# Modulation weights before rows in the first stage, and rows turned by products with diag(1/norm)

## The chip, the core and the metric

The kernel runs on one core of a Trainium2 chip. The time is device microseconds (us) of one execution, the median over the runs. The core has TensorE (PE, matrix products), VectorE (DVE), ScalarE (ACT), GpSimd (POOL), SyncE (SP, which here issues the loads) and DMA engines, all running on their own and tied by semaphores.

## The reference

One block of a hybrid network: four sequence mixers over 1,280 tokens (256 of context, 1,024 of the sequence; 1,024 channels), and then a mixture of experts. What matters here is how the mixers' input is made:

```python
def rms_norm(x, g):
    xf = x.astype(jnp.float32)
    y = xf * lax.rsqrt(jnp.mean(xf * xf, axis=-1, keepdims=True) + RMS_EPS)
    return (y * g.astype(jnp.float32)).astype(x.dtype)

def modulate(x, g, shift, scale):
    return rms_norm(x, g) * (1 + scale) + shift
...
        mod_x = jax.nn.silu(c) @ w_mod[i] + b_mod[i]
        mod_c = jax.nn.silu(c_ctx) @ w_mod[i] + b_mod[i]
        sa_x, ca_x, ga_x, sf_x, cf_x, gf_x = jnp.split(mod_x[:, None, :], 6, axis=-1)
        sa_c, ca_c, ga_c, sf_c, cf_c, gf_c = jnp.split(mod_c[None, None, :], 6, axis=-1)
        y_c, ctx_states = mixer_block(modulate(ctx, norm1_g[i], sa_c, ca_c), ctx_init, lp, 1, n_ctx)
        y_x, _ = mixer_block(modulate(x, norm1_g[i], sa_x, ca_x), ctx_states, lp, rows, GRID_W)
```

## The kernel before, in words

All data are float32. The kernel is a chain of stages, each a `Phase` that ends with a barrier of all engines. The first stage is `front`, the second `gla` (one of the mixers); seven more follow, in which the change alters nothing.

`front` makes `k.hT`, the modulated input with channels on the partitions: 8 chunks of 128 channels by 1,280 tokens. The tokens come as ten tiles `X[:, t]` of 128 rows by 1,024 channels, two of context and eight of the sequence. The order on each engine is the order in which the code is written.

- SP loads the two conditions `c` and `c_ctx`, the ten row tiles (512 KB each), the first two of the six sections of `w_mod` in eight loads of 1 MB (two loads, a piece of 2 MB, for each pair of the eight chunks of input channels), and the vectors `b_mod` and `norm1_g`.
- ACT takes the Silu of the conditions and then sums the squares of each row tile (line 248).
- DVE makes the reciprocal roots for five tiles at a time (`rsqrt`, twelve dependent small instructions after line 291 has formed the means) and scales the five tiles in place with them (line 294). This is done twice.
- PE multiplies the conditions with each weight piece as it lands (line 264, four output strips), turns the result into columns (line 270) after DVE has copied it out (line 297), and DVE forms the gain and shift columns (lines 303 to 309). Then PE turns the scaled rows by transposes (line 281), in three groups of two, four and four tiles, eight channel chunks each, chunk `c_` into bank `c_`. ACT evicts banks 0 to 3 (line 253) and DVE banks 4 to 7 (line 314), applying gain and shift. A bank is refilled when its last eviction is out.

In `gla`, SP loads the low-rank weights `WG`, four loads of the q/k weights `W[0]`, the gate weights, and the v/g weights `W[1]`. PE computes the low-rank products (line 473: 512, 512 and 256 tokens), which DVE evicts (line 665), and then the q/k products (line 516).

Of the kernel before, what the change touches and what calls it, by code (L numbers as in the profile page):

```python
# [70 lines left out]
class Chain:  # L71
# [123 lines left out]
def front(nc, k, ctx, cr, x, ctx_in, c, c_ctx, w_mod, b_mod, norm1_g):  # L195
# [9 lines left out]
        sem("mod_rows_done"), sem("mod_rows_out"), sem("mod_columns_turned"), sem("mod_columns_out"), sem("front_chain"))  # L205
    W = cr.take(2, KC, D)
    X = cr.take(NT, D)
    R = cr.take(512)
    sc = cr.take(KC, 32)
    cc = cr.take(2, KC)  # L210
    bcol, gcol, modc = cr.take(6, KC), cr.take(KC), cr.take(2, KC, 2)
    ss, rs, ri, rt = (cr.take(NT) for _ in range(4))
    junk = k.hT[:, 0, 0:D]
    ps = k.ps
    wv = w_mod[0].rearrange("(p c) (s n) -> s p c n", c=KC, s=6)
    tiles = [ctx_in[0, t * P:(t + 1) * P, :] for t in range(CT)] + [x[0, t * P:(t + 1) * P, :] for t in range(XT)]
    BATCH = NT // 2
    groups = [(1, 0, CT), (0, CT, CT + 4), (0, CT + 4, NT)]
    by_channel = lambda w, c_, h: w[:, c_, :].rearrange("p (q m) -> p m q", m=KC)[:, 4 * h:4 * h + 4, :]
    with nc.Block() as block:  # L220
# [17 lines left out]

        @block.scalar
        def _(act):  # L240
            act.wait_ge(c_in, 32)
            act.wait_ge(zeroed, 1)
            nc.scalar.activation(sc[:, :, 0:2].rearrange("p c j -> p j c"), cc, ACT.Silu).then_inc(act_in, 1)
            for t in range(NT):
                act.wait_ge(x_in[t], 16)
                if t >= 1:
                    act.wait_ge(sq, t)
                nc.scalar.activation(junk, X[:, t], ACT.Square, accum_out=ss[:, t:t + 1]).then_inc(sq, 1)
            act.wait_ge(cols_out, 4)
            for g, (j, a, b) in enumerate(groups):  # L250
# [33 lines left out]
        @block.vector  # L284
        def _(dve):
            chain = Chain(dve, vch)

            for n in range(2):
                b = slice(n * BATCH, (n + 1) * BATCH)
                dve.wait_ge(sq, (n + 1) * BATCH)  # L290
                chain(nc.vector.tensor_scalar(rs[:, b], ss[:, b], 1.0 / D, RMS_EPS, ALU.mult, ALU.add))
                rsqrt(nc, chain, rs[:, b], ri[:, b], rt[:, b])
                for t in range(n * BATCH, (n + 1) * BATCH):
                    nc.vector.tensor_scalar(X[:, t], X[:, t], ri[:, t:t + 1], None, ALU.mult).then_inc(xn_ready, 1)
# [16 lines left out]
            for g, (j, a, b) in enumerate(groups):  # L311
                for c_ in range(KC // 2, KC):
                    dve.wait_ge(turned, g * KC + c_ + 1)
                    nc.vector.tensor_scalar(k.hT[:, c_, a * P:b * P], ps[c_][:, 0:(b - a) * P],
                                            k.mul_col[0][j][:, c_:c_ + 1], k.add_col[0][j][:, c_:c_ + 1],
                                            ALU.mult, ALU.add).then_inc(out[1], 1)
# [57 lines left out]
def gla(nc, k, ctx, cr, w_in, gate_w2, gate_b, norm_g, ahead):  # L374
# [6 lines left out]
    W0 = cr.take(KC, 2 * GW)  # L381
# [8 lines left out]
    WG, low_end = cr.take(KC, 32), cr.at  # L390
# [8 lines left out]
    wg_in, qk_in, vg_in, w2_in = (sem("low_w_loaded"), [sem(f"qk_w_{c}_loaded") for c in range(KC // 2)],  # L399
                                  sem("vg_w_loaded"), sem("gate_w_loaded"))  # L400
# [33 lines left out]
    with nc.Block() as block:  # L434
        @block.sync
        def _(sp):
            sp.dma_start(WG, view[:, :, A_GL:A_GL + 32]).then_inc(wg_in, 16)
            for c in range(KC // 2):
                cs = slice(2 * c, 2 * c + 2)
                sp.dma_start(W[0][:, cs], view[:, cs, A_Q:A_Q + 2 * GW]).then_inc(qk_in[c], 16)  # L440
# [26 lines left out]
        def _(pe):  # L467
            pe.wait_ge(wg_in, 16)
# [38 lines left out]
            for p in range(NPROD):  # L507
# [5 lines left out]
                for c in range(KC):  # L513
                    if p == 0 and c % 2 == 0:
                        pe.wait_ge(qk_in[c // 2], 16)
                    last = nc.tensor.matmul(k.ps[p % 4][:, 0:width], k.hT[:, c, t * P:(t + 1) * P], W[g][:, c, ws],  # L516
                                            start=(c == 0), stop=(c == KC - 1))
# [2636 lines left out]
class Turn:  # L3154
# [556 lines left out]
def block_kernel(nc, io, out):  # L3711
    ctx = ExitStack()
    with ctx:
# [27 lines left out]
        with Phase(nc) as c:  # L3741
            left = gla(nc, k, c, at(free), io["w_in"], io["gla_gate_w2"], io["gla_gate_b"], io["gla_norm_g"], for_mamba)
# [58 lines left out]
```

## Time and profile before

| | us |
|---|---|
| Time, median of 3 runs | 2637.87 (2637.47 to 2639.95) |
| Profiled execution, its time | 2639.51 |
| Its span, first to last instruction | 2637.8 |
| Last square starts | 16.99 |
| Fourth burst of modulation products starts | 37.58 |
| Turning of rows starts, ends | 44.05, 53.25 |
| First product of `gla` starts | 58.93 |
| First q/k product starts | 67.87 |

Starts are counted from the span's start. "PE idle" in a row is the time before the instruction in which the engine had nothing to do, with the instruction or transfer that ended it. A float32 product is listed as two MATMUL records, a transpose as one. Over the whole span the mean granted clock of TensorE is 0.968 of full speed.

### The profile page before, as it was taken

How to read it: one execution, taken by the hardware profiler on the slowest of the kernel's cores; microseconds unless marked ns; L12 is line 12 of the kernel's file. 1: busy time of each engine (PE TensorE's matmuls, PEld its weight loads, DVE VectorE, ACT ScalarE, POOL GpSimd, SP SyncE). 2: the span in 40 equal slices, each digit the busy share in tenths (PEclk: the TensorE clock that was granted, in tenths of full speed). 3: DMA queues.
4: the chain of work that ended last, by engine and by line, in shares of the span. 5: the costliest groups of instructions: out<-in, count | busy, mean ns of one | idle time of the engine just before them, and what ended most of it. 6: DMA issues, size and time to landing. Idle time of an engine off the chain costs nothing. (4 is left out here: it accounts for less than half of the span.)

```text
span 2637.8 us, 72412 instructions
## 1 busy us (share of the span) xinstructions
PE 2434.2 (92%) x27309; PEld 1316.8 (50%) x27310; DVE 1504.5 (57%) x2601; ACT 967.0 (37%) x1642; POOL 827.8 (31%) x655
## 2 busy tenths in 40 slices
PE   4998999999799898999697978999999999999977
PEld 2446458555799455999443443333333333333333
DVE  3106556754577424676434855666666666666538
ACT  3513116312222123333111134555555555555422
POOL 1000000000454001111000035566666666666564
PEclk9999999999999999999798989999999999999988
DMA  6001312130000200000322277899989898693177
GB/s 249 26 0 53 129 32 68 49 112 1 13 4 4 56 12 1 4 4 4 122 93 80 88 293 286 336 351 365 352 311 363 325 336 333 231 337 131 66 297 300
DMA packets 109435, 410.21 MB, mean 156 GB/s; under 512 B 20954, under 2 KB 37036, under 8 KB 84141
## 3 DMA queue, kind: packets, MB, share of 16 engines
q1 hardware_dynamic: 76972, 289.81, 30.1%
q0 software_dynamic: 20736, 75.51, 7.4%
q10 hardware_dynamic: 11520, 41.95, 4.1%
q8 instruction: 154, 2.52, 0.4%
q14 instruction: 53, 0.43, 0.1%
HBM read 347.45 MB, written 59.77 MB: 154 GB/s over the span
## 5 line engine op out<-in xcount | busy, mean ns | idle before, releaser
L3367 PE MATMUL bank<-arena 128*32 x1280 | 570.2, 599 | 11.9 <-SPq L68 8.0
L3369 PE MATMUL bank<-arena 128*32 128x512 f32 x3840 | 571.3, 599 | 0.0
L3328 POOL COPY arena<-arena 128x2048 f32 x240 | 448.8, 1903 | 335.9 <-PE bank L3401 314.6
L3367 PEld LDWEIGHTS bank<-arena 128*32 128x32 f32 x1280 | 135.1, 110 | 362.0 <-issue 353.1
L3398 PE MATMUL bank<-arena 128*32 x640 | 290.4, 597 | 5.5 <-POOL arena L3328 5.5
L3401 PE MATMUL bank<-arena 128*32 128x512 f32 x1920 | 291.4, 597 | 0.0
L3522 DVE COPY arena<-arena 128x2048 f32 x80 | 133.6, 1670 | 208.9 <-PE bank L3369 190.8
L3459 ACT COPY arena<-arena 128x2048 f32 x80 | 152.0, 1900 | 176.7 <-PE bank L3369 149.7
L3318 POOL DMA_INDIRECT arena<-normed_rows,arena x80 | 164.0, 2050 | 119.2 <-DVE arena L3506 107.4
L1313 PE MATMUL bank<-arena 64*64 64x64 f32 x4480 | 164.8, 219 | 12.5 <-DVE arena L1385 5.4
L3398 PEld LDWEIGHTS bank<-arena 128*32 128x32 f32 x640 | 70.6, 110 | 198.5 <-issue 197.5
L1313 PEld LDWEIGHTS bank<-arena 64*64 64x64 f32 x4480 | 150.3, 135 | 17.9 <-DVE arena L1385 6.5
L3465 ACT COPY arena<-arena 128x2048 f32 x80 | 151.9, 1898 | 0.0
L3369 PEld LDWEIGHTS bank<-arena 128*32 128x32 f32 x3840 | 151.1, 110 | 0.0
L3500 DVE TENSOR_SCALAR arena<-bank,arena 128x128 f32<-128x128 f32 x320 | 109.3, 404 | 40.7 <-PE bank L3352 40.7
L1554 PE MATMUL bank<-arena 128*128 128x512 f32 (+1 forms) x320 | 132.0, 569 | 0.0
L516 PE MATMUL bank<-arena 128*128 128x512 f32 (+1 forms) x320 | 127.3, 552 | 0.0
L3434 ACT ACTIVATE arena<-bank,arena 128x128 f32<-128x128 f32 x320 | 120.9, 465 | 3.5 <-PE bank L3352 3.5
L2552 POOL TENSOR_TENSOR arena<-arena 128x512 f32<-128x512 f32 x10 | 12.8, 1282 | 345.3 <-DVE arena L2618 231.6
L1432 DVE SCALAR_TENSOR_TENSOR arena<-arena 128x945 f32<-128x945 f32 (+2 forms) x96 | 113.8, 1220 | 1.7
L2837 PE MATMUL bank<-arena 128*128 128x512 f32 x256 | 112.0, 595 | 0.0
L1385 DVE TENSOR_TENSOR arena<-arena,bank 128x512 f32<-128x512 f32 x100 | 68.5, 685 | 68.3 <-PE bank L1313 67.7
(558 smaller groups left out, 4327.5 us busy)
## 6 DMA issues: line engine op xcount, KB each, us to landing
arena<-in_exp_w_gate_dram SPq DMA_DIRECT2D x64, 1024.0 KB, 6.2
arena<-in_exp_w_up_dram SPq DMA_DIRECT2D x64, 1024.0 KB, 8.7
arena<-in_exp_w_down_dram SPq DMA_DIRECT2D x64, 1024.0 KB, 9.7
expert_rows<-arena ACTq DMA_DIRECT2D x80, 512.0 KB, 8.6
arena<-in_w_mod_dram SPq DMA_DIRECT2D x32, 512.0 KB, 4.4
arena<-in_x_dram SPq DMA_DIRECT2D x16, 512.0 KB, 5.6
arena<-in_w_mod_dram SPq DMA_DIRECT2D x8, 1024.0 KB, 18.5
arena<-in_w_in_dram SPq DMA_DIRECT2D x4, 1536.0 KB, 10.2
```

The source lines that it names most:

```text
L516: last = nc.tensor.matmul(k.ps[p % 4][:, 0:width], k.hT[:, c, t * P:(t + 1) * P], W[g][:, c, ws], start=(c == 0), stop=(c == KC - 1))
L1313: last = self.nc.tensor.matmul(self.banks[bank][r, x * HD:(x + 1) * HD], lhsT[r, x], rhs[r, x], start=True, stop=True)
L1554: last = nc.tensor.matmul(k.ps[p % 4][:, 0:w], W[m // 3 % 2][:, c, (m % 3) * P:(m % 3 + 1) * P], k.hT[:, c, a:a + w], start=(c == 0), stop ...
L3318: nc.gpsimd.indirect_dma_start(out=G[:, b.q], out_offset=None, in_=xn_dram, in_offset=bass.IndirectOffsetOnAxis(ap=ID[:, b.q], axis=0)).th ...
L3328: last = nc.gpsimd.tensor_copy(down_copy(u), down_of(slots[u]))
L3367: nc.tensor.matmul(out(SUB - 1), XTT[:, b.q, c, rows(SUB - 1)], W[:, :, c], start=first, stop=end)
L3369: last = nc.tensor.matmul(out(u), XTT[:, b.q, c, rows(u)], WC[:, u, :, c], start=first, stop=end)
L3398: nc.tensor.matmul(ps[6 + half][rows(SUB - 1), :], HT[:, b.q, f, rows(SUB - 1)], W[:, f, c], start=(f == 0), stop=(f == 1))
L3401: last = nc.tensor.matmul(ps[6 + half][rows(u), :], HT[:, b.q, f, rows(u)], WDC[:, u, f, c], start=(f == 0), stop=(f == 1))
L3459: nc.scalar.copy(copy_of(2, LOW), part_of(slot, LOW)).then_inc(lo_a, 1)
L3465: nc.scalar.copy(copy_of(2, HIGH), part_of(slot, HIGH)).then_inc(hi_a, 1)
L3522: nc.vector.tensor_copy(copy_of(0, LOW), part_of(slots[0], LOW))
```

## The change

In `front`, SP now issues the modulation weights and the two vectors first, then the ten row tiles, and then weights for `gla`: the low-rank weights at once, and the four q/k loads when the modulation products are done. For this the buffers of rows and small tiles get other places in the arena, and `gla` gets its `WG` and `W0` from outside. The rows are no longer scaled. DVE instead makes for each tile a 128x128 diagonal `DG[:, t]` of reciprocal norms, and PE turns and scales a tile in one product of `X[:, t, c_::KC]` with it. The tiles are in four groups of 2, 3, 3 and 2 instead of three; ACT and DVE do the squares and reciprocals of group g+1 before they evict group g, and DVE forms no reciprocals before the modulation columns are out.

```diff
     W = cr.take(2, KC, D)
-    X = cr.take(NT, D)
-    R = cr.take(512)
...
-    junk = k.hT[:, 0, 0:D]
+    X = Carve(cr.arena, cr.at + 3 * D + 80).take(NT, D)
+    R, junk, DG = small.take(512), small.take(D), small.take(NT, P)
...
-    BATCH = NT // 2
-    groups = [(1, 0, CT), (0, CT, CT + 4), (0, CT + 4, NT)]
+    groups = [(1, 0, CT), (0, CT, CT + 3), (0, CT + 3, CT + 6), (0, CT + 6, NT)]
...
-            for t in range(NT):
-                sp.dma_start(X[:, t], tiles[t]).then_inc(x_in[t], 16)
             for c_ in range(KC // 2):
                 cs = slice(2 * c_, 2 * c_ + 2)
                 for s in range(2):
                     sp.dma_start(W[:, s, cs], wv[s][:, cs]).then_inc(first_in[c_], 16)
             sp.dma_start(bcol, b_mod.rearrange("a (s p c) -> p (a s) c", s=6, c=KC)).then_inc(vec_in, 16)
             sp.dma_start(gcol, norm1_g.rearrange("a (p c) -> p (a c)", c=KC)).then_inc(vec_in, 16)
+            for t in range(NT):
+                sp.dma_start(X[:, t], tiles[t]).then_inc(x_in[t], 16)
+            sp.dma_start(next_low, view[:, :, A_GL:A_GL + 32]).then_inc(next_in, 16)
+            sp.wait_ge(rows_done, 1)
+            for c_ in range(KC // 2):
+                cs = slice(2 * c_, 2 * c_ + 2)
+                sp.dma_start(next_w[:, cs], view[:, cs, A_Q:A_Q + 2 * GW]).then_inc(next_in, 16)
+            sp.wait_ge(next_in, 16 * (1 + KC // 2))
...
+            squares(*groups[0][1:])
+            act.wait_ge(cols_out, 4)
+            for g in range(len(groups)):
+                if g + 1 < len(groups):
+                    squares(*groups[g + 1][1:])
+                leave(g)
...
                     for t in range(a, b):
-                        last = nc.tensor.transpose(ps[c_][:, (t - a) * P:(t - a + 1) * P], X[:, t, c_::KC], k.ident)
+                        last = nc.tensor.matmul(ps[c_][:, (t - a) * P:(t - a + 1) * P], X[:, t, c_::KC], DG[:, t],
+                                                start=True, stop=True)
                     last.then_inc(turned, 1)
...
-            for n in range(2):
-                b = slice(n * BATCH, (n + 1) * BATCH)
-                dve.wait_ge(sq, (n + 1) * BATCH)
-                chain(nc.vector.tensor_scalar(rs[:, b], ss[:, b], 1.0 / D, RMS_EPS, ALU.mult, ALU.add))
-                rsqrt(nc, chain, rs[:, b], ri[:, b], rt[:, b])
-                for t in range(n * BATCH, (n + 1) * BATCH):
-                    nc.vector.tensor_scalar(X[:, t], X[:, t], ri[:, t:t + 1], None, ALU.mult).then_inc(xn_ready, 1)
+            def normed(a, b):
+                dve.wait_ge(sq, b)
+                n = slice(a, b)
+                chain(nc.vector.tensor_scalar(rs[:, n], ss[:, n], 1.0 / D, RMS_EPS, ALU.mult, ALU.add))
+                rsqrt(nc, chain, rs[:, n], ri[:, n], rt[:, n])
+                for t in range(a, b):
+                    nc.vector.tensor_scalar(DG[:, t], k.ident, ri[:, t:t + 1], None, ALU.mult).then_inc(xn_ready, 1)
...
+            normed(*groups[0][1:])
+            for g in range(len(groups)):
+                if g + 1 < len(groups):
+                    normed(*groups[g + 1][1:])
+                leave(g)
...
-def gla(nc, k, ctx, cr, w_in, gate_w2, gate_b, norm_g, ahead):
+def gla(nc, k, ctx, cr, w_in, gate_w2, gate_b, norm_g, own, ahead):
...
         def _(sp):
-            sp.dma_start(WG, view[:, :, A_GL:A_GL + 32]).then_inc(wg_in, 16)
-            for c in range(KC // 2):
-                cs = slice(2 * c, 2 * c + 2)
-                sp.dma_start(W[0][:, cs], view[:, cs, A_Q:A_Q + 2 * GW]).then_inc(qk_in[c], 16)
             sp.wait_ge(w2_zero, 1)
```

Here is SP's queue from the conditions to the first loads of `gla`, before:

```order
L229 DMA arena<-in_c_ctx_dram 128x8
L231 DMA arena<-in_ctx_dram 128x1024 x2
L231 DMA arena<-in_x_dram 128x1024 x8
L235 DMA arena<-in_w_mod_dram 128x2x1024 x8
L236 DMA arena<-in_b_mod_dram 128x6x8
L237 DMA arena<-in_norm_g_dram 128x8
L220 UNCONDITIONAL_BRANCH
L435 UNCONDITIONAL_BRANCH [waits barrier_Pool_Activation_PE_DVE_SP_release]
L437 DMA arena<-in_w_in_dram 128x8x32
L440 DMA arena<-in_w_in_dram 128x2x512 x4
```

and with the change:

```order
L230 DMA arena<-in_c_ctx_dram 128x8
L234 DMA arena<-in_w_mod_dram 128x2x1024 x8
L235 DMA arena<-in_b_mod_dram 128x6x8
L236 DMA arena<-in_norm_g_dram 128x8
L238 DMA arena<-in_ctx_dram 128x1024 x2
L238 DMA arena<-in_x_dram 128x1024 x8
L239 DMA arena<-in_w_in_dram 128x8x32
L243 DMA arena<-in_w_in_dram 128x2x512 [waits mod_rows_done]
L243 DMA arena<-in_w_in_dram 128x2x512 x3
L221 UNCONDITIONAL_BRANCH [waits next_weights_loaded]
L462 UNCONDITIONAL_BRANCH [waits barrier_Pool_Activation_PE_DVE_SP_release]
```

The ten row loads moved behind ten others, and the five weight loads of `gla` from behind the barrier to before it.

ACT's queue from the last squares to the end of `front`, before (a bank of 256 or 512 columns is an eviction):

```order
L248 ACTIVATE arena<-arena 128x1024 [waits squares_summed,x_8_loaded]
L248 ACTIVATE arena<-arena 128x1024 [waits squares_summed,x_9_loaded]
L253 ACTIVATE arena<-bank,arena 128x256 [waits x_turned,mod_columns_out]
L253 ACTIVATE arena<-bank,arena 128x256 [waits x_turned] x3
L253 ACTIVATE arena<-bank,arena 128x512 [waits x_turned] x8
```

and with the change, from the third square on:

```order
L257 ACTIVATE arena<-arena 128x1024 [waits squares_summed,x_2_loaded,mod_columns_out]
L257 ACTIVATE arena<-arena 128x1024 [waits squares_summed,x_3_loaded]
L257 ACTIVATE arena<-arena 128x1024 [waits squares_summed,x_4_loaded]
L263 ACTIVATE arena<-bank,arena 128x256 [waits x_turned] x4
L257 ACTIVATE arena<-arena 128x1024 [waits squares_summed,x_5_loaded]
L257 ACTIVATE arena<-arena 128x1024 [waits squares_summed,x_6_loaded]
L257 ACTIVATE arena<-arena 128x1024 [waits squares_summed,x_7_loaded]
L263 ACTIVATE arena<-bank,arena 128x384 [waits x_turned] x4
L257 ACTIVATE arena<-arena 128x1024 [waits squares_summed,x_8_loaded]
L257 ACTIVATE arena<-arena 128x1024 [waits squares_summed,x_9_loaded]
L263 ACTIVATE arena<-bank,arena 128x384 [waits x_turned] x4
L263 ACTIVATE arena<-bank,arena 128x256 [waits x_turned] x4
```

Eight of the ten squares moved behind the modulation columns, between the evictions.

DVE's queue at the start of `front`, before, where the norms stand first:

```order
L291 TENSOR_SCALAR arena<-arena 128x5 [waits squares_summed]
L111 TENSOR_SCALAR arena<-arena 128x5 [waits front_chain]
L112 TENSOR_SCALAR arena<-arena 128x5 [waits front_chain]
L114 TENSOR_TENSOR arena<-arena 128x5 [waits front_chain]
L115 SCALAR_TENSOR_TENSOR arena<-arena 128x5 [waits front_chain]
```

and with the change, where the copy of the modulation rows and the columns do:

```order
L325 COPY arena<-bank 128x512 [waits mod_rows_done,mod_vectors_loaded,identity_made]
L331 TENSOR_TENSOR arena<-bank,arena 128x8 [waits mod_columns_turned]
L331 TENSOR_TENSOR arena<-bank,arena 128x8 x3
L335 SCALAR_TENSOR_TENSOR arena<-arena 128x8 [waits front_chain]
L337 COPY arena<-arena 128x8
L335 SCALAR_TENSOR_TENSOR arena<-arena 128x8
L337 COPY arena<-arena 128x8
L309 TENSOR_SCALAR arena<-arena 128x2 [waits squares_summed,mod_columns_out]
L111 TENSOR_SCALAR arena<-arena 128x2 [waits front_chain]
```

The norms moved behind the columns, and come in batches of 2, 3, 3 and 2 tiles.

## Rows read from the trace of the kernel before

**Rows 1.** Timeline, SP's queue: start us, us, engine, line, what it issues.
```profile
6.67 14.72 SPq L235 DMA_DIRECT2D arena<-in_w_mod_dram  x8
...
23.99 7.16 SPq L237 DMA_DIRECT2D arena<-in_norm_g_dram  x1
...
55.81 0.67 SPq L437 DMA_DIRECT2D arena<-in_w_in_dram  x1
```

**Rows 2.** Timeline of TensorE: start us, us, ..., count [idle before it <- who ended it].
```profile
22.22 3.88 PE L264 MATMUL bank<-arena 128*32 128x512 f32 x16 [22.22 <-DMA arena<-in_w_mod_dram]
...
37.58 3.86 PE L264 MATMUL bank<-arena 128*32 128x512 f32 x16 [1.35 <-DMA arena<-in_w_mod_dram]
...
44.05 9.20 PE L281 MATMUL bank<-arena 128*128 128x128 f32 x80 [1.00 <-DVE arena L309]
...
58.93 9.01 PE L473 MATMUL bank<-arena 128*32 128x512 f32 x48 [5.67 <-DMA arena<-in_w_in_dram]
...
67.87 3.72 PE L516 MATMUL bank<-arena 128*128 128x256 f32 x16
```

**Rows 3.** Timeline, last squares (ACT), second batch of norms and scalings (DVE).
```profile
15.70 1.06 ACT L248 ACTIVATE arena<-arena 128x1024 f32<-128x1024 f32 x1
...
16.99 1.06 ACT L248 ACTIVATE arena<-arena 128x1024 f32<-128x1024 f32 x1
...
18.17 0.17 DVE L291 TENSOR_SCALAR arena<-arena 128x5 f32<-128x5 f32 x1 [0.47 <-ACT arena L248]
...
20.58 3.41 DVE L294 TENSOR_SCALAR arena<-arena 128x1024 f32<-128x1024 f32 x5
```

**Rows 4.** Busy time by stretch; last three columns: granted clock, DMA share, GB/s.
```profile
37.00:53.30 16.30, 13.69 (x100) 9.91 (x100) 7.69 (x19) 7.50 (x12) 0.00 (x0) 1.00 0.01 2
53.30:58.90 5.60, 0.00 (x0) 0.00 (x0) 3.81 (x9) 0.00 (x0) 0.57 (x3) 0.82 0.33 53
58.90:63.80 4.90, 4.87 (x18) 1.13 (x20) 0.00 (x0) 0.00 (x0) 0.00 (x0) 0.51 0.99 352
63.80:67.90 4.10, 4.10 (x34) 1.38 (x29) 1.37 (x2) 0.00 (x0) 0.00 (x0) 1.00 1.06 347
```

**Rows 5.** Timeline, evictions of turned rows and VectorE's next start.
```profile
44.61 4.74 ACT L253 ACTIVATE arena<-bank,arena 128x256 f32<-128x256 f32 x8 [26.47 <-PE bank L281]
...
51.95 2.97 DVE L314 TENSOR_SCALAR arena<-bank,arena 128x512 f32<-128x512 f32 x4 [0.63 <-PE bank L281]
...
56.01 0.48 DVE L655 MEMSET arena<- 96x512 f32 x1 [1.09 <-PEq L136]
```

**Rows 6.** Timeline, VectorE evicts the low-rank products, 512 tokens each.
```profile
64.12 0.69 DVE L665 COPY arena<-bank 96x512 f32<-96x512 f32 x1 [5.55 <-PE bank L473]
...
66.70 0.69 DVE L665 COPY arena<-bank 96x512 f32<-96x512 f32 x1 [1.89 <-PE bank L473]
```

**Rows 7.** Timeline of TensorE, products of 128x128 float32 in a later stage.
```profile
427.15 1.06 PE L1053 MATMUL bank<-arena 128*128 128x128 f32 x4
428.00 1.06 PE L1077 MATMUL bank<-arena 128*128 128x128 f32 x4
...
429.81 0.61 PE L1053 MATMUL bank<-arena 128*128 128x128 f32 x4
430.25 0.61 PE L1077 MATMUL bank<-arena 128*128 128x128 f32 x4
```

**Rows 8.** Busy time by stretch of these products, and after a barrier (265.5).
```profile
265.50:268.00 2.50, 2.50 (x16) 0.81 (x12) 2.47 (x2) 2.36 (x3) 0.00 (x0) 0.50 0.13 20
426.90:428.60 1.70, 1.70 (x10) 1.70 (x9) 0.28 (x2) 1.70 (x9) 0.00 (x0) 0.50 1.07 392
429.80:430.90 1.10, 1.06 (x10) 0.87 (x8) 0.80 (x3) 1.10 (x5) 0.00 (x0) 1.00 1.05 352
```

**Rows 9.** Timeline of TensorE around the next stage boundary.
```profile
261.06 0.64 PE L594 MATMUL bank<-arena 64*64 64x64 f32 x30
264.12 2.70 PE L865 MATMUL bank<-arena 128*32 128x512 f32 x16 [2.42 <-PEq L136]
```

More of the change, by code:

```diff
@@ L192, in constants, with front @@
     pool.wait_ge(made, n)
-def front(nc, k, ctx, cr, x, ctx_in, c, c_ctx, w_mod, b_mod, norm1_g):
+def front(nc, k, ctx, cr, small, x, ctx_in, c, c_ctx, w_mod, b_mod, norm1_g, w_in, ahead):
     sem = lambda n: ctx.semaphore(n)
@@ L205, in front @@
         sem("mod_rows_done"), sem("mod_rows_out"), sem("mod_columns_turned"), sem("mod_columns_out"), sem("front_chain"))
+    next_in = sem("next_weights_loaded")
+    next_low, next_w = ahead
     W = cr.take(2, KC, D)
-    X = cr.take(NT, D)
-    R = cr.take(512)
[L209 to L212, printed above, removed]
-    junk = k.hT[:, 0, 0:D]
+    X = Carve(cr.arena, cr.at + 3 * D + 80).take(NT, D)
+    R, junk, DG = small.take(512), small.take(D), small.take(NT, P)
+    sc = small.take(KC, 32)
+    cc = small.take(2, KC)
+    bcol, gcol, modc = small.take(6, KC), small.take(KC), small.take(2, KC, 2)
+    ss, rs, ri, rt = (small.take(NT) for _ in range(4))
     ps = k.ps
     wv = w_mod[0].rearrange("(p c) (s n) -> s p c n", c=KC, s=6)
+    view = w_in[0].rearrange("(p c) n -> p c n", c=KC)
     tiles = [ctx_in[0, t * P:(t + 1) * P, :] for t in range(CT)] + [x[0, t * P:(t + 1) * P, :] for t in range(XT)]
-    BATCH = NT // 2
-    groups = [(1, 0, CT), (0, CT, CT + 4), (0, CT + 4, NT)]
+    groups = [(1, 0, CT), (0, CT, CT + 3), (0, CT + 3, CT + 6), (0, CT + 6, NT)]
     by_channel = lambda w, c_, h: w[:, c_, :].rearrange("p (q m) -> p m q", m=KC)[:, 4 * h:4 * h + 4, :]
@@ L243, in _, with squares, leave @@
             nc.scalar.activation(sc[:, :, 0:2].rearrange("p c j -> p j c"), cc, ACT.Silu).then_inc(act_in, 1)
[L244 to L250, printed above, removed]
+            def squares(a, b):
+                for t in range(a, b):
+                    act.wait_ge(x_in[t], 16)
+                    if t >= 1:
+                        act.wait_ge(sq, t)
+                    nc.scalar.activation(junk, X[:, t], ACT.Square, accum_out=ss[:, t:t + 1]).then_inc(sq, 1)
+            def leave(g):
+                j, a, b = groups[g]
                 for c_ in range(KC // 2):
@@ L286, in _, with leave @@
             chain = Chain(dve, vch)
-            for n in range(2):
-                b = slice(n * BATCH, (n + 1) * BATCH)
-                dve.wait_ge(sq, (n + 1) * BATCH)
-                chain(nc.vector.tensor_scalar(rs[:, b], ss[:, b], 1.0 / D, RMS_EPS, ALU.mult, ALU.add))
-                rsqrt(nc, chain, rs[:, b], ri[:, b], rt[:, b])
-                for t in range(n * BATCH, (n + 1) * BATCH):
-                    nc.vector.tensor_scalar(X[:, t], X[:, t], ri[:, t:t + 1], None, ALU.mult).then_inc(xn_ready, 1)
+            def normed(a, b):
[3 more added lines that the diff above has]
+                rsqrt(nc, chain, rs[:, n], ri[:, n], rt[:, n])
+                for t in range(a, b):
+                    nc.vector.tensor_scalar(DG[:, t], k.ident, ri[:, t:t + 1], None, ALU.mult).then_inc(xn_ready, 1)
+            def leave(g):
+                j, a, b = groups[g]
+                for c_ in range(KC // 2, KC):
+                    dve.wait_ge(turned, g * KC + c_ + 1)
+                    nc.vector.tensor_scalar(k.hT[:, c_, a * P:b * P], ps[c_][:, 0:(b - a) * P],
+                                            k.mul_col[0][j][:, c_:c_ + 1], k.add_col[0][j][:, c_:c_ + 1],
+                                            ALU.mult, ALU.add).then_inc(out[1], 1)
+            dve.wait_ge(ident_made, 1)
             dve.wait_ge(vec_in, 32)
@@ L310, in _ @@
             dve.wait_ge(cols_out, 4)
[L311 to L316, printed above, removed]
+            normed(*groups[0][1:])
[3 more added lines that the diff above has]
+                leave(g)
 def write_out(sp, y, y_dram, m, written):
@@ L380, in gla @@
     DEC = cr.take(2, NT, 2, 2)
-    W0 = cr.take(KC, 2 * GW)
+    WG, W0 = own
+    cr.take(KC, 2 * GW)
     O = W0.rearrange("p (d t) (s n) -> p d (t s) n", d=2, s=2)
@@ L389, in gla @@
     CH, DS = cr.take(4 * NT), cr.take(2 * GW)
-    WG, low_end = cr.take(KC, 32), cr.at
+    cr.take(KC, 32)
     W = W0, cr.take(KC, 2 * GW)
@@ L397, in gla @@
     ROW = 32 * LOW
-    wg_in, qk_in, vg_in, w2_in = (sem("low_w_loaded"), [sem(f"qk_w_{c}_loaded") for c in range(KC // 2)],
-                                  sem("vg_w_loaded"), sem("gate_w_loaded"))
+    vg_in, w2_in = sem("vg_w_loaded"), sem("gate_w_loaded")
     w2_zero, ones_set, ch_zero, ch_made, s_zero, gm_made = (sem("gate_w_zeroed"), sem("ones_row_set"),
@@ L3733, in block_kernel @@
         at = lambda a: Carve(arena, a)
+        for_gla = at(45752).take(KC, 32), at(30864).take(KC, 2 * GW)
         with Phase(nc) as c:
-            front(nc, k, c, at(free), io["x"], io["ctx"], io["c"], io["c_ctx"], io["w_mod"], io["b_mod"],
-                  io["norm1_g"])
+            front(nc, k, c, at(free), at(46264), io["x"], io["ctx"], io["c"], io["c_ctx"], io["w_mod"], io["b_mod"],
+                  io["norm1_g"], io["w_in"], for_gla)
         dn_left = at(48704).take(2 * XT, 2, HD), at(50752).take(2, SEQ)
```

6 lines of the change are left out of this document (2 added, 4 removed).

## The prediction, made before the changed kernel was run

> **What bounds the kernel now.** I read the queue of loads first, then TensorE's rows, then ScalarE's and VectorE's, and last the clock. The change touches only the first stage and the start of the second, so I ask what ends each piece of the first 68 us. The reader is to see three serial pieces. First, loads: SP issues ten row tiles and then eight loads of modulation weights, the last of these only at about 21 us [rows 1], and TensorE's four bursts of modulation products start as the pieces land, the first at 22.22 and the fourth at 37.58 [rows 2]. Each piece (two loads) takes (37.58 - 22.22) / 3 = 5.12 us, each burst 3.86. Squares and norms are long done by then: the last square starts at 16.99, and VectorE has scaled its second batch by 20.58 + 3.41 = 24.0 [rows 3]. Second, with no load under way (DMA share 0.01 from 37 to 53.3 [rows 4]), TensorE turns all rows from 44.05 to 53.25 [rows 2], and the last eviction ends at 51.95 + 2.97 = 54.92 [rows 5]. Third, the next stage has to load its weights: TensorE sits idle 5.67 us and starts at 58.93 [rows 2]. It starts slowly: the granted clock is 0.51 (the 1.2 GHz level) from 58.9 to 63.8 and 1.00 after [rows 4], so the first 512 tokens of the low-rank products, evicted at 64.12, took 5.19 us, where the next 512 took 66.70 - 64.12 = 2.58 [rows 6]. Everything later begins with the first q/k product at 67.87 [rows 2]. That moment is my measuring point: from there to the end I take before and after as equal, since the later code is the same.
>
> **The change, part by part.**
>
> *Loads.* The ten row tiles hold 5 MB and a modulation piece 2 MB, so the pieces lose 2.5 pieces of waiting: 2.5 x 5.12 = 12.8 us. The last burst starts at 37.58 - 12.8 = 24.8 and ends at 28.7. From its start to the first turn was 44.05 - 37.58 = 6.47 us [rows 2]; that chain (bank copy, four transposes, sums, gains) is unchanged, so the modulation columns are ready at about 31.1. The total loaded before the last row is the same, so the last row lands where the last piece did, at about 38, and tile t at 38 - 1.28 x (9 - t). The two small vectors are now ahead of the rows. Their issue took 7.16 us for the second [rows 1], behind a full queue; that issue was through at 31.15, six microseconds before the last piece landed [rows 1, 2], so by then the queue still held that much work, and the rows are issued before it runs dry. Price 0, and about 2 us if that cover were gone: the rows that ScalarE needs at 31.2 to 33.7 land at 29 to 32.
>
> *Norms.* The ten scalings by VectorE (3.41 us for five, [rows 3]) were hidden under loads: removing them gives 0. But the reciprocals come onto the path. One batch takes 20.58 - 18.17 = 2.41 us whatever its width [rows 3], and there are now four batches, all behind the columns. Scaling a 128x128 diagonal is in no row: at most the 0.68 us of a 1024-element one, at least the 0.17 us that a 5-element instruction is listed with [rows 3]. I take 0.15 to 0.2 at the pace of a pipelined row, nearer the low end, since the data are an eighth. First product: 31.1 + 2.4 + 0.3 + 0.15 for the semaphore = 34.0.
>
> *Turning by products.* A transpose costs 9.20 / 80 = 0.115 us [rows 2]. A float32 product of this size is listed twice, and two of them take 430.25 - 429.81 = 0.44 us at clock 1.00 and 428.00 - 427.15 = 0.85 at 0.50 [rows 7, 8]: 0.22 and 0.43 each. The strided rows may add a little (the transposes read the same stride at 0.115 a pass), so I take 0.23. Which clock? TensorE will have done four transposes between 28.7 and 34.0, and before a gap of this kind (5.67 us) brought it down [rows 2, 4], so it starts low. It came back 63.8 - 58.9 = 4.9 us after work began [rows 4]. By that, 4.8 us at 0.43 make 11 products, and the other 69 take 69 x 0.23 = 15.9: the last ends at 34.0 + 4.8 + 15.9 = 54.7, if nothing else holds it. ScalarE: from 31.2, eight squares at 16.99 - 15.70 = 1.29, and sixteen evictions, about 8.8 us (eight, of 256 and 512 columns, took 4.74 [rows 5]), free at about 50. VectorE: four times 2.4, ten diagonals, evictions of 8.9 (0.74 for 512 columns [rows 5], narrower ones in between): free at about 51 to 52 with its waits for squares. So TensorE becomes the bound of this stage, by some 3 us, and its last bank is evicted 0.3 + 0.55 later, at 55.6. Against 54.92 that is a loss of 0.7 us: the overlap with the loads is eaten by slower turning and by reciprocals on the path.
>
> *Next weights.* They are asked for at about 31 and land about 5 us behind the last row, near 45, ten us before the stage ends. TensorE then need not wait for a load after the barrier. VectorE started 56.01 - 54.92 = 1.09 after the last eviction [rows 5]; I take 1.0 for TensorE, so 56.6 against 58.93: a gain of 2.3.
>
> *Clock at the start of the next stage.* TensorE's gap is 56.6 - 54.7 = 1.9 us instead of 5.67. If the clock stays up, the low-rank products take 2.58 where they took 5.19 in the first 512 tokens: about 2.5 us more. The gate weights are issued behind the barrier as before, with an empty queue, and are wanted 10 us later: 0.
>
> **Sum.** -0.7 for the later last eviction, + 3.0 for the way from there to TensorE's next start (4.0 before, 1.0 after), + 2.5 for the clock: the first q/k product at 67.87 - 4.8 = 63.1. The profiled execution took 2639.51 for a span of 2637.8, and lies 1.6 above the median of the runs, 2637.87; applied to the median, 2637.87 - 4.8 = 2633.1. A measurement of this kernel can tell about 0.2%, 5.3 us, from no change, so the forecast lies just inside "no change".
>
> **Bounds.** The clock may return after 3 to 6.5 us of work, an estimate around the 4.9 seen: each microsecond at the low level costs 1 - 0.23/0.43 = 0.46, so plus or minus 0.8. Diagonals, semaphores and the pace of strided products: plus or minus 0.8 together. Own range of this case: 2631.5 to 2634.8.
>
> A row and a rule on the clock: through 9.2 us of nothing but transposes the granted clock is 1.00, and it falls only in the idle stretch after them [rows 2, 4]. The Trainium skill, "TensorE: Matmul & The Clock Gate", Part 4, says that transposes do not count as work for the clock. By the trace they keep it up and the gap brings it down, so a gap may do so again (rival B keeps its chance); by the rule products would hold the clock where transposes did not, and rival B would be all but out, with the same sum.
>
> **The rivals.**
> A, the forecast, 2633.1: chance 0.50.
> B, the clock falls again at the barrier. For it: at the next such barrier TensorE was idle from 261.70 to 264.12, 2.4 us after sparse work, and the clock was 0.50 at 265.5 [rows 8, 9]. Against: here the work before the gap is dense. It costs 1 to 2.5 us: 2634 to 2635.6. Chance 0.20.
> C, the clock stays up through the wait for the first diagonals. Against: the 5.3 us with half a microsecond of work. Then all 80 products take 18.4 us from 34.0, VectorE's chain of reciprocals and evictions becomes the bound near 53.7, and the gain is 4.8 + 1.9 = 6.7: 2631.2. Chance 0.14.
> D, the other side: the clock stays low while products come in groups with waits between. Then 80 x 0.43 = 34.2 us, turning ends at 68.2, the next stage starts at 70.1 and its first part takes the slow 8.9: 79.0 against 67.87, 2649. It decides at 15 us of low clock (4.8 + 4.8/0.46), where the gain is gone, and at 27 us the kernel is slower by 0.2%. For it: a product costs twice a transpose. Against: low, TensorE is so slow that it never waits, and unbroken work raised the clock in 4.9 us. The Trainium skill, "Perfetto Trace Analysis", section Transposes, wants logical transposes done as transposes and not as standard matmuls, which speaks for D and gives no time. Chance 0.07.
> E, the gain is lost: the rows come 4 us or more later than worked out, or a later stage waits for something not moved: about 2638. Chance 0.09.
>
> **How the numbers follow.** Faster by over 0.2% is C, about two fifths of A: 0.35. Slower is D and a rest: 0.08. Within: 0.57. The range takes in C with 1.4 below it, B, and E with 1.8 above, and leaves D out: 2629.8 to 2639.8.
>
> **What the next profile would show.** Modulation bursts from about 9.4 on, the last at 24.8; the columns at 31.1; products from 34.0 with a low clock until about 39, then without gaps to 54.7; evictions ending at 55.6; low-rank products starting at 56.6 with clock 1.00 and first evicted 2.6 us later. Wrong would be: rows landing after 40; a first product much after 34; a clock of 0.5 over the whole turning; TensorE waiting for diagonals in the later groups, which would make VectorE the bound; or a low clock from 57 on.

## The result, and the profile after

The changed kernel took 2651.94 us (median of 5 runs, 2647.94 to 2655.45) against 2637.87 before: 1.0052 times as long, 95% interval 1.0041 to 1.0063. That is 14.1 us slower, where 4.8 us faster was forecast, and above the range. The profiled execution took 2655.45, its span 2653.5 (2637.8 before), mean granted clock 0.969 (0.968).

TensorE's timeline of the changed kernel, the counterpart of [rows 2]:

```profile
9.65 3.88 PE L281 MATMUL bank<-arena 128*32 128x512 f32 x16 [9.65 <-DMA arena<-in_w_mod_dram]
...
25.31 3.86 PE L281 MATMUL bank<-arena 128*32 128x512 f32 x16 [1.66 <-DMA arena<-in_w_mod_dram]
30.19 0.63 PE L287 MATMUL bank<-arena 128*128 128x128 f32 x4 [1.01 <-DVE arena L325]
34.62 38.34 PE L298 MATMUL bank<-arena 128*128 128x128 f32 x160 [3.80 <-DVE arena L312]
74.49 8.02 PE L495 MATMUL bank<-arena 128*32 128x512 f32 x48 [1.53 <-PEq L136]
```

The first two rows are the first and the last modulation burst: the loads came half a microsecond later than worked out. The turning then starts early, at 34.62 where it was 44.05, and runs without a gap, but takes 38.34 us for 160 passes: 0.24 a pass, 0.48 a product. It ends at 72.96, where the transposes ended at 53.25. The first q/k product starts at 82.44, 14.6 us later than [rows 2], and the span ends 15.7 later: the loss is made in the first stage.

The busy time by stretch of the same kernel (granted clock is the third column from the end):

```profile
34.60:41.00 6.40, 6.38 (x27) 6.38 (x27) 3.55 (x17) 4.51 (x9) 0.00 (x0) 0.60 1.07 360
41.00:73.00 32.00, 31.96 (x135) 31.76 (x134) 13.25 (x44) 11.63 (x20) 0.00 (x0) 1.00 0.09 33
...
74.40:77.50 3.10, 3.01 (x12) 0.88 (x14) 2.19 (x6) 0.00 (x0) 0.57 (x3) 0.53 0.08 19
```

The clock is not the cause: 27 passes took 6.4 us at 0.60 (0.50 until 39 us) and 135 took 32.0 at 1.00, 0.24 each at either level. So what bounds a pass here doesn't follow that clock. And the weight loader (PEld) is busy all the time beside the products. VectorE's last evictions wait for TensorE at a steady beat:

```profile
70.14 0.55 DVE L318 TENSOR_SCALAR arena<-bank,arena 128x256 f32<-128x256 f32 x1 [4.08 <-PE bank L298]
71.09 0.54 DVE L318 TENSOR_SCALAR arena<-bank,arena 128x256 f32<-128x256 f32 x1 [0.41 <-PE bank L298]
72.04 0.55 DVE L318 TENSOR_SCALAR arena<-bank,arena 128x256 f32<-128x256 f32 x1 [0.41 <-PE bank L298]
73.00 0.54 DVE L318 TENSOR_SCALAR arena<-bank,arena 128x256 f32<-128x256 f32 x1 [0.41 <-PE bank L298]
```

A bank of the last group holds two products, four passes, and the starts are 0.95 apart: 0.238 a pass. This spacing is the ruler for the experiments below; it needs no count of TensorE's records.

### The profile page after: what moved, and what is told of

Its sections match the earlier page's. It is cut to its first block and busy times, and to the rows that moved or that the text cites. A ratio compares the mean times of both kernels' runs of the same rounds, so it can differ in the third digit from the quotient of the medians.

```text
span 2653.5 us, 72605 instructions
## 1 busy us (share of the span) xinstructions
PE 2461.2 (93%) x27389; PEld 1348.0 (51%) x27390; DVE 1505.5 (57%) x2629; ACT 970.2 (37%) x1646; POOL 829.2 (31%) x655
## 5 line engine op out<-in xcount | busy, mean ns | idle before, releaser
L3387 PE MATMUL bank<-arena 128*32 x1280 | 568.8, 598 | 14.1 <-SPq L68 8.3
L1333 PEld LDWEIGHTS bank<-arena 64*64 64x64 f32 x4480 | 150.4, 135 | 18.4 <-DVE arena L1405 6.5
## 6 DMA issues: line engine op xcount, KB each, us to landing
arena<-in_w_mod_dram SPq DMA_DIRECT2D x8, 1024.0 KB, 14.1
```

The source lines that it names most:

```text
L1333: last = self.nc.tensor.matmul(self.banks[bank][r, x * HD:(x + 1) * HD], lhsT[r, x], rhs[r, x], start=True, stop=True)
L3387: nc.tensor.matmul(out(SUB - 1), XTT[:, b.q, c, rows(SUB - 1)], W[:, :, c], start=first, stop=end)
```

## The experiments

Theory S: the product pays for the step at which it reads the rows. `X[:, t, c_::KC]` takes every eighth float32, 32 bytes apart. Theory P: the product itself costs this wherever its rows lie. Besides them stands the question what the other halves of the change (order, next weights ahead) are worth. The runs of the kernel before beside these experiments had medians of 2637.11 (19 runs, 2632.55 to 2647.17; beside e1 to e4), 2638.51 (17 runs, 2629.89 to 2645.17; beside e5 to e7) and 2634.25 (one run; beside e8 and e9). In four experiments (e1, e5, e6 and e9) other channels stand in `k.hT` than the reference's, and in one (e8) the rows aren't turned. The loads of the expert stage depend on the data: from its first to its last product it takes 987 to 991 us in these five and 970 to 977 in all other kernels here. So of these five the first stage and its boundary are read, and their whole times are only named.

**Contiguous rows** (e1_contig, against the changed kernel):

```diff
- ...matmul(ps[c_][...], X[:, t, c_::KC], DG[:, t], ...
+ ...matmul(ps[c_][...], X[:, t, c_ * P:(c_ + 1) * P], DG[:, t], ...
```

> The changed kernel with one edit: the stationary operand of the turning products is 128 neighbouring channels instead of every eighth (a step of 32 bytes), so the channels of hT are permuted. Theory S (step): a float32 product reads a stationary operand with that step at about 0.24 us a pass whatever the clock, and without it at 0.11 a pass at the high clock. Then the turning products, 38.3 us in the profile after, take about 20 to 22 us with some waits for diagonals, the first q/k product of the next stage starts at 63 to 65 us instead of 82.4, and the time is 2633 to 2638. Theory P (any product in this place, whatever its step, is slow, for instance because its moving operand changes every time): 38 us again and about 2652.

TensorE's timeline of this run, then its groups of one form (count | busy us, mean ns):

```profile
34.62 20.95 PE L298 MATMUL bank<-arena 128*128 128x128 f32 x160 [3.81 <-DVE arena L312]
57.12 6.64 PE L495 MATMUL bank<-arena 128*32 128x512 f32 x48 [1.55 <-PEq L136]
63.69 0.48 PE L536 MATMUL bank<-arena 128*128 128x256 f32 x1
```

```profile
L298 PE MATMUL bank<-arena 128*128 128x128 f32 x160 | 20.9, 300 | 3.8 <-DVE arena L312 3.8
L298 PEld LDWEIGHTS bank<-arena 128*128 128x128 f32 x160 | 20.8, 216 | 4.0 <-DVE arena L312 4.0
```

The same 160 passes from the same start take 20.95 us instead of 38.34, and the clock now tells: between 34.6 and 41 us (clock 0.53) 31 passes, between 41 and 55 (1.00) 128 passes, 0.11 each. In the changed kernel one weight load took 335 ns on the mean, here 216. The first q/k product starts at 63.69. S holds, P falls. The whole time, 2651.12 us (4 runs, 2649.74 to 2654.91), missed the 2633 to 2638 that were expected; the last part of this section takes that up.

**Order and next weights alone** (e2_order_only, against the changed kernel):

```diff
- ...matmul(ps[c_][...], X[:, t, c_::KC], DG[:, t], start=True, stop=True)
+ ...transpose(ps[c_][...], X[:, t, c_::KC], k.ident)
...
- nc.vector.tensor_scalar(DG[:, t], k.ident, ri[:, t:t + 1], None, ALU.mult)
+ nc.vector.tensor_scalar(X[:, t], X[:, t], ri[:, t:t + 1], None, ALU.mult)
```

> The changed kernel's order of loads, squares and norms, but VectorE scales the rows in place (0.68 us a tile) and TensorE turns them by transposes, as before the change. S and P both expect transposes at 0.115 us each where they are not waiting, about 9 to 10 us in sum, so that the product is shown to be the whole loss. What is left is the order alone: four chains of reciprocals of 2.4 us and the scalings stand on the path behind the modulation columns. By my chain the first q/k product starts at 65.5 to 67.5 against 67.87 before the change: 2635 to 2638, that is the same or just faster than before. A theory that the order of loads itself costs (rows late) expects over 2642.

2631.15 us (10 runs, 2628.19 to 2633.18): 0.9976 of before, 0.9967 to 0.9986. Its TensorE timeline:

```profile
35.39 3.67 PE L298 MATMUL bank<-arena 128*128 128x128 f32 x16 [4.74 <-DVE arena L311]
39.77 2.95 PE L298 MATMUL bank<-arena 128*128 128x128 f32 x24 [0.70 <-DVE arena L311]
46.13 4.55 PE L298 MATMUL bank<-arena 128*128 128x128 f32 x24 [3.42 <-DVE arena L311]
52.17 2.83 PE L298 MATMUL bank<-arena 128*128 128x128 f32 x16 [1.49 <-DVE arena L311]
57.21 8.02 PE L494 MATMUL bank<-arena 128*32 128x512 f32 x48 [2.21 <-PEq L136]
65.16 1.13 PE L535 MATMUL bank<-arena 128*128 128x256 f32 x4
```

With transposes TensorE waits before each group for VectorE's scaled rows: VectorE is the bound, as the forecast had it for case C. Even so the first q/k product starts 17.3 us earlier than in the changed kernel. The loss is the product's. Mark and time lie a little below what was expected (65.5 to 67.5, and 2635 to 2638).

**The product alone** (e3_product_only, against the kernel before: `transpose(..., X[:, t, c_::KC], k.ident)` becomes `matmul(..., X[:, t, c_::KC], k.ident, start=True, stop=True)`):

> The kernel before the change with one edit: the transposes of the rows become products with the identity, same operands, same step of 32 bytes. Theory S expects 160 passes of 0.24 us, 38 us instead of 9.2, at a granted clock of 1.00, so about 29 us more: 2667. Theory P in the form that the freshly written, changing diagonal is at fault expects 0.115 a pass with the constant identity: 18.4 us and 2647. A theory that the low clock made the loss expects at most 18.4 us as well, since here the clock is up when turning starts.

One run, 2664.46 us. Its TensorE timeline:

```profile
44.16 38.35 PE L281 MATMUL bank<-arena 128*128 128x128 f32 x160 [1.00 <-DVE arena L310]
87.77 7.93 PE L474 MATMUL bank<-arena 128*32 128x512 f32 x48 [5.25 <-DMA arena<-in_w_in_dram]
95.63 1.56 PE L517 MATMUL bank<-arena 128*128 128x256 f32 x6
```

38.35 us again, with no diagonal in it and no load under way (DMA share 0.00): neither fresh right-hand operands nor transfers cost anything here. The turning takes 29.15 us longer, and the first q/k product starts 27.8 later than [rows 2]. The clock wasn't at 1.00 throughout, as the expectation had it, but 0.72 in the mean from 44 to 50 us, which at this step costs nothing either.

**Next weights ahead alone** (e4_ahead_only: the kernel before, in whose first stage SP issues, behind `norm1_g`, the low-rank weights, and after the modulation products the four q/k loads; buffers as in the change):

> The kernel before the change, only that the low-rank and q/k weights of the second stage are loaded at the end of the first (with the buffers where the change puts them); order of rows, norms and transposes are as before. Expected: TensorE starts the second stage about 1.5 us after the last eviction instead of 4.0, a gain of 2.5, and if the clock stays up over the shorter gap another 2.5: 2633 to 2635.5. Rival: the clock falls anyway, gain 2.5 alone: 2635.4. Rival: a load was hidden anyway or later waits swallow it: 2638.

2633.57 us (10 runs, 2628.57 to 2637.70): 0.9987, 0.9974 to 0.9999. Its TensorE timeline:

```profile
45.09 9.23 PE L290 MATMUL bank<-arena 128*128 128x128 f32 x80 [1.00 <-DVE arena L318]
56.94 8.19 PE L477 MATMUL bank<-arena 128*32 128x512 f32 x48 [2.61 <-PEq L136]
65.05 1.13 PE L518 MATMUL bank<-arena 128*128 128x256 f32 x4
```

TensorE's idle time before the low-rank products falls from 5.67 to 2.61 us, and the first q/k product comes 2.8 us earlier, as early as with the new order as well (65.16). The order of loads adds nothing at this mark, since the turning waits for VectorE instead. Whether it adds something to the whole time isn't settled: the intervals of the two kernels overlap, with the median of "order alone" 2.4 us lower.

**Where the price sets in** (e5_steps_products, against the changed kernel; groups of 2, 3, 3, 2 tiles read their rows at steps of 8, 1, 2 and 4 elements):

```diff
+ by_step = lambda t, c_, s: X[:, t, (c_ // s) * P * s + c_ % s:min(D, (c_ // s + 1) * P * s):s]
...
- ...matmul(ps[c_][...], X[:, t, c_::KC], DG[:, t], ...
+ ...matmul(ps[c_][...], by_step(t, c_, (8, 1, 2, 4)[g]), DG[:, t], ...
```

> The changed kernel, whose four groups of turning products now read their stationary operand with steps of 8, 1, 2 and 4 elements (32, 4, 8 and 16 bytes), so that the channels of hT are permuted in part. By e1 the step is what costs. Two forms of that theory: a cost of a far step alone, so that 8 and 16 bytes stay at 0.11 us a pass and only 32 bytes takes 0.24; or a cost that grows with the step, or sets in at 16 bytes. The first group should show 0.24 (at the low and the high clock alike), the second 0.11 at the high clock and 0.21 at the low. Only the paces are read from this run, not its time.

Busy time of this run in a stretch inside each group:

```profile
34.70:42.20 7.50, 7.50 (x32) 7.50 (x32) 4.28 (x18) 5.63 (x11) 0.00 (x0) 0.77 1.07 365
42.50:47.50 5.00, 5.00 (x47) 5.00 (x46) 4.52 (x19) 4.52 (x9) 0.00 (x0) 1.00 0.27 99
48.70:53.20 4.50, 4.50 (x41) 4.50 (x40) 3.95 (x16) 2.62 (x4) 0.00 (x0) 1.00 0.00 0
54.00:60.90 6.90, 6.90 (x31) 6.81 (x30) 1.89 (x4) 2.26 (x4) 0.00 (x0) 1.00 0.01 2
```

Steps of 1 and 2 run at the full pace, and step 4 is nearly as slow as step 8. By the spacing of evictions that waited for TensorE: step 8, 0.95 for four passes; step 2, 0.71 for six, 0.118 each; step 4, (57.31 - 54.51) / 3 = 0.933 for four, 0.233 each, from these rows:

```profile
54.51 0.56 ACT L264 ACTIVATE arena<-bank,arena 128x256 f32<-128x256 f32 x1 [3.08 <-PE bank L299]
...
57.31 0.56 ACT L264 ACTIVATE arena<-bank,arena 128x256 f32<-128x256 f32 x1 [0.37 <-PE bank L299]
```

One load took 192 ns on the mean in the second stretch, 196 in the third, 329 in the fourth.

**The same steps with transposes** (e6_steps_transposes, that edit in the kernel of "order alone"):

> The kernel of e2 (order of the change, rows scaled by VectorE, transposes) with the same four steps: 8, 1, 2 and 4 elements. If a transpose is indifferent to the step, all groups show 0.115 us each at the high clock and 0.21 to 0.23 at the low one. If it only hides half of the cost, the unit-step group shows less than 0.115, toward 0.06, at the high clock. Only the paces are read from this run.

Its TensorE timeline, where the second, third and fourth row have steps 1, 2 and 4:

```profile
35.78 3.67 PE L299 MATMUL bank<-arena 128*128 128x128 f32 x16 [4.73 <-DVE arena L312]
40.15 4.54 PE L299 MATMUL bank<-arena 128*128 128x128 f32 x24 [0.69 <-DVE arena L312]
46.51 4.62 PE L299 MATMUL bank<-arena 128*128 128x128 f32 x24 [1.83 <-DVE arena L312]
52.55 2.85 PE L299 MATMUL bank<-arena 128*128 128x128 f32 x16 [1.41 <-DVE arena L312]
```

Against step 8 throughout (order alone: 3.67, 2.95, 4.55, 2.83) the third and fourth groups agree to 0.07. The second is slower with contiguous rows, 4.54, but its clock was 0.61 in the mean of that stretch where it was 1.00 there; the third group of "order alone", as many transposes at step 8 and a clock of 0.62, took 4.55. These groups are slowed by the low clock or by waits, so the pace at the full clock is read from the end of the second group, TensorE's instructions of line 299 alone (count of PE, count of PEld, clock):

```profile
43.70:44.50 0.80, 0.80 (x9) 0.75 (x7) 1.00 0.30 82
```

The contiguous transposes start there 0.11 us apart, as those at step 8 do at clock 1.00, and not 0.06. By the same starts steps 2 and 4 take about 0.12. A transpose hardly feels the step.

**Other steps** (e9_steps_more, steps 8, 3, 6 and 5 from 64-byte boundaries):

```diff
+ by_step = lambda t, c_, s: X[:, t, (c_ if s == 8 else 16 * c_):][:, 0:127 * s + 1:s]
...
+ ...matmul(ps[c_][...], by_step(t, c_, (8, 3, 6, 5)[g]), DG[:, t], ...
```

> The rows are read at a step of 8, 3, 6 and 5 elements in the groups of 2, 3, 3 and 2 tiles, each from a 64-byte boundary, where the run before this had 8, 1, 2 and 4; other channels than the reference's then stand in k.hT. Step 2 ran at 0.118 us a pass and step 4 at 0.234. If what is paid for is a new 16-byte line for each element, steps 5 and 6 cost 0.234 like 4 and 8, and step 3, of which every fourth element lies in the line of the one before it, lies in between, 0.17 to 0.21. If the cost grows with the bytes walked, steps 5 and 6 differ from 4 and 8, which they did not from each other (0.234 and 0.24). If there is only a limit above step 2, step 3 costs 0.234 too. Group 2 is read off the windows at clock 1.00.

ScalarE's timeline of this run, two neighbouring evictions of the second, third and fourth group (six, six and four passes each):

```profile
45.21 0.67 ACT L264 ACTIVATE arena<-bank,arena 128x384 f32<-128x384 f32 x1 [0.37 <-PE bank L299]
46.25 0.67 ACT L264 ACTIVATE arena<-bank,arena 128x384 f32<-128x384 f32 x1 [0.37 <-PE bank L299]
...
52.79 0.67 ACT L264 ACTIVATE arena<-bank,arena 128x384 f32<-128x384 f32 x1 [2.55 <-PE bank L299]
54.12 0.67 ACT L264 ACTIVATE arena<-bank,arena 128x384 f32<-128x384 f32 x1 [0.66 <-PE bank L299]
...
63.02 0.56 ACT L264 ACTIVATE arena<-bank,arena 128x256 f32<-128x256 f32 x1 [5.55 <-PE bank L299]
63.91 0.56 ACT L264 ACTIVATE arena<-bank,arena 128x256 f32<-128x256 f32 x1 [0.33 <-PE bank L299]
```

Step 3 costs 1.04 / 6 = 0.173 a pass, step 6 1.33 / 6 = 0.222, step 5 0.89 / 4 = 0.222. Step 3 lies in between, and steps of 4, 5, 6 and 8 within 8% of each other. That fits a price for each new 16-byte piece of memory, and not one for the distance walked: at step 3 three of four elements begin a new piece, and 3/4 of the 0.233 of step 4 is 0.175, against 0.173; at step 2 half of them do, 0.117 against 0.118. At step 1 the same count would give 0.06, but the pass takes 0.11, so there something else bounds it. That 4 and 8 cost a little more than 5 and 6 this doesn't explain.

The Trainium skill, "SBUF — State Buffer", in its note on cachelines, says that memory is read in 16-byte lines, that two accesses to a line are needed for the full rate, and that this allows four float32 of step for free. These runs agree with the first two statements (steps 1 and 2 at full pace, each element on its own line slow), not with the last: four elements are already at the full price.

**Which operand** (e8_moving, against the changed kernel: `matmul(..., X[:, t, c_::KC], DG[:, t], ...)` becomes `matmul(..., DG[:, t], X[:, t, c_::KC], ...)`, so that the diagonal is loaded and the rows stream):

> The two operands of the turning product change places: the diagonal is loaded, and the rows X[:, t, c_::8] stream past it. The tile is then scaled but not turned, so that k.hT holds other values; the place, number, shape and float type of the products are those of the changed kernel. Theory S in its narrow form (only the loading of a stationary operand pays for a 32-byte step): 0.11 us a pass where the clock is 1.00, the turning takes 20 to 22 us and the next stage starts near 57. Theory S in its wide form (whichever operand is read at that step pays; the modulation bursts, whose moving operand has the same step, took 3.86 us for 16 records where the low-rank products took 2.58): 0.2 to 0.24 us a pass, the turning 33 to 39 us. I give the narrow form 0.35 and the wide form 0.65.

TensorE's groups of this form in this run:

```profile
L298 PE MATMUL bank<-arena 128*128 128x128 f32 x160 | 37.7, 413 | 3.8 <-DVE arena L312 3.8
L298 PEld LDWEIGHTS bank<-arena 128*128 128x128 f32 x160 | 33.7, 220 | 7.6 <-DVE arena L312 4.0
```

The turning takes 37.7 us, though one load now takes 220 ns like a contiguous one. At a step of 8 either operand pays; the narrow form of S falls. Swapping the operands is no way out.

**A version on the other side** (e7_split_rows: transposes; six row tiles ahead of the modulation weights and four behind; groups of 2, 4, 4; all squares before the evictions; ACT evicts five banks; next weights ahead). Its core against "order alone", with `EARLY` set to `CT + 4`:

```diff
+            for t in range(EARLY):
+                sp.dma_start(X[:, t], tiles[t]).then_inc(x_in[t], 16)
             for c_ in range(KC // 2):
...
-            for t in range(NT):
+            for t in range(EARLY, NT):
...
+            normed(0, EARLY)
             dve.wait_ge(vec_in, 32)
```

> A version that combines what paid: next weights ahead, transposes, rows scaled by VectorE, but six row tiles before the modulation weights and four behind them, three groups of 2, 4 and 4, all squares first, the last norms between the evictions of the first and second group, and ScalarE taking five banks of eight. The first six tiles' norms are hidden again, the columns are ready at 39 instead of 43.9, the last row lands at 38 and only one chain of reciprocals stands on the path. Sum: last eviction at 50.5 to 52, first q/k product at 58.5 to 60 against 67.87 before: 2628 to 2630 beside a before of 2637.5, ratio 0.9965. Rival: VectorE, with 2.4 us of reciprocals and 2.7 of scaling between evictions, holds up TensorE and the low clock returns at the barrier: 2632.

2632.76 us (12 runs, 2629.13 to 2640.82): 0.9981, 0.9968 to 0.9993. Its TensorE timeline:

```profile
39.51 5.63 PE L300 MATMUL bank<-arena 128*128 128x128 f32 x48 [1.00 <-DVE arena L338]
47.75 5.44 PE L300 MATMUL bank<-arena 128*128 128x128 f32 x32 [2.61 <-DVE arena L313]
55.53 6.64 PE L495 MATMUL bank<-arena 128*32 128x512 f32 x48 [2.34 <-PEq L136]
62.09 3.72 PE L536 MATMUL bank<-arena 128*128 128x256 f32 x16
```

It has the earliest first q/k product of all, 5.8 us before [rows 2], and about 5.8 us less time than the kernel before beside it. Against "order alone" the time isn't told apart: of the 3 us that it leads at the mark, the whole time keeps none that can be measured. All three kernels with transposes and next weights ahead beat both the kernel before and the changed one.

**From the mark to the end.** The forecast takes everything behind the first q/k product as equal. This table has, from one profile of each kernel, the start of that product, of the first product of the third stage (`mamba`) and of the expert stage, and the length of the expert stage from its first to its last product, in us:

| kernel | q/k | `mamba` | experts | their length | span |
|---|---|---|---|---|---|
| before | 67.9 | 264.1 | 1542.0 | 976.9 | 2637.8 |
| changed | 82.4 | 283.0 | 1558.6 | 974.8 | 2653.5 |
| contiguous rows (e1) | 63.7 | 263.6 | 1543.0 | 990.2 | 2653.2 |
| order alone (e2) | 65.2 | 262.2 | 1537.9 | 971.3 | 2629.3 |
| next weights alone (e4) | 65.1 | 262.1 | 1538.2 | 970.3 | 2630.2 |
| split rows (e7) | 62.1 | 258.2 | 1536.3 | 970.4 | 2630.7 |

The kernel with contiguous rows leads the changed one by 18.8 us at the mark and by 15.6 at the experts, and loses that lead in the expert stage, where its data are others. But it also leads the kernel before by 4.2 us at the mark, and of that 0.5 is left at `mamba` and nothing at the experts. In part the granted clock fell in the second stage where it had not before, 0.78 against 1.00 in the same piece of the work (before, then contiguous rows):

```profile
220.00:225.00 5.00, 4.36 (x104) 3.74 (x103) 4.89 (x19) 3.15 (x8) 0.00 (x0) 1.00 1.05 340
215.80:220.80 5.00, 5.00 (x85) 4.39 (x83) 4.42 (x16) 2.71 (x6) 0.00 (x0) 0.78 1.05 338
```

The changed kernel lost another 4.3 us between the mark and `mamba` and regained 2 behind it. Why is open, and one profile of a kernel can't tell such shifts from chance. A lead of a few microseconds at the mark is therefore not yet one in the time.

## Why the prediction was wrong

*The step that failed* is the price of the product: "The strided rows may add a little (the transposes read the same stride at 0.115 a pass), so I take 0.23". It is 0.48. Both rows behind it were real and neither had both properties at once: the products of [rows 7] cost 0.22 at clock 1.00 but read contiguous operands, and the transposes read at the step but aren't products. With contiguous rows the forecast's own arithmetic comes true up to the mark: 20.95 us where it said 20.7, first q/k product at 63.69 where it said 63.1. Whether the 4.8 us would then have shown in the time isn't known: in the one profile of that kernel the lead over the kernel before is gone by the experts. The bounds allowed 0.8 us for "the pace of strided products" together with two other things, and so took in none of this: a bound from the nearest row, [rows 2], was at hand but not drawn. There 16 passes of 512 columns, whose moving operand has this very step, take 3.86 us; 16 passes of 512 contiguous columns take 2.58 [rows 6]. A ratio of 1.5 for strided products would have put about 10 us on the turning (an estimate, half of 20.7), well outside the range, though still short of the 17.6 that it cost.

*How the miss adds up*, at the first q/k product, forecast 63.1, measured 82.44: first product at 34.62 instead of 34.0, +0.6; turning 38.34 instead of 20.7, +17.6; from its end to the next stage 1.53 instead of 1.9, -0.4; low-rank products 7.95 instead of 6.5, +1.5. Together that is the whole 19.3.

*What held.* Last burst at 25.31 (24.8), columns at about 31.7 (31.1), two diagonals in 0.48 us where 0.3 was worked out, first product within 0.6, TensorE as the bound of the stage, no wait for a load behind the barrier, and a low clock at the first products. That low clock would have cost 2.3 us as worked out (20.7 against 80 x 0.23 = 18.4), and about 3 in the contiguous run (31 passes in 6.4 us, which at 0.11 take 3.4); at a step of 8 it cost nothing, since a pass took 0.24 anyway.

*The rivals.* D gave 68.2 for the end of the turning and 2649 for the time; measured were 72.96 and 2651.94. It was nearest in outcome, by another mechanism: it had the clock low throughout at 0.43 a product, while the clock was 1.00 from 41 us on. B was half right beside it: the clock did fall at the barrier again, 0.53 from 74.4 to 77.5, for some 1.4 us.

*The rules weighed there.* The Trainium skill, "Perfetto Trace Analysis", section Transposes, wanted transposes and no standard products here. These runs bear it out, with a size: 9.2 us against 38.35 for the same tiles. That factor of four is two factors of two: a product is two passes where a transpose is one, and at this step a pass takes 0.24 instead of 0.11. The other rule is that of the Trainium skill, "TensorE: Matmul & The Clock Gate", Part 4: transposes don't count as work for the clock. From it the prediction drew that products would hold the clock where transposes didn't. The runs show neither half: the clock fell after the products of the changed kernel (0.53 from 74.4) and stayed at 1.00 after the transposes of the kernel with split rows, and in "order alone" it rose while TensorE did nothing but transposes, 0.50 and then 1.00:

```profile
35.39:39.10 3.71, 3.67 (x16) 3.27 (x16) 3.30 (x15) 2.97 (x6) 0.00 (x0) 0.50 1.08 336
39.77:42.72 2.95, 2.94 (x24) 2.75 (x24) 2.69 (x10) 2.86 (x7) 0.00 (x0) 1.00 1.05 387
```

## What to carry to other kernels

Before a transpose is replaced by a product, look at the step of the operand it reads: in float32 a product here paid about double for rows whose elements lie 16 bytes or more apart (as the moving operand tried at 32 bytes alone), and the transpose did not. A row shows a price for one kind of operation and one access pattern together; where the changed code joins two properties that no row has together, neither row bounds it, and the range must hold the product of both. The work worth keeping of this change was the quiet part, loads for the next stage issued before the barrier, 3.5 us of 2637 by the medians, with an interval from 0.3 to 6.9.

## What the runs showed of the hardware, unexpected

- A float32 128x128 pass at clock 1.00 takes 0.11 to 0.118 us at steps of 1 and 2 elements, 0.173 at 3, 0.222 at 5 and 6, 0.233 to 0.24 at 4 and 8, and at step 8 the same at either clock level.
- A transpose of the same tile takes 0.11 to 0.12 at steps of 1, 2, 4 and 8. Why it is spared isn't settled; no run here takes it apart.
- After the same idle time of 1.53 to 1.55 us with dense products ahead, the clock fell to 0.53 in the changed kernel (low-rank products 8.02 us) and stayed up with contiguous rows (6.64); after transposes it stayed up over 2.34 us in the kernel with split rows (6.64) and fell to 0.50 over 2.21 us in "order alone" (8.02). The length of a gap alone doesn't decide it, and what does stays open.
